# One core of a streaming encoder: the differential-attention layers rebuilt as one pipeline over all heads

## The reference, cut to what matters

```python
s = jnp.einsum('bqhmd,bkhmd->bhmqk', q, k, preferred_element_type=jnp.float32) * (A_DK ** -0.5)
s = s + jnp.transpose(bias, (2, 3, 0, 1))[None]      # T5 bias, constant from a distance of 128 on
if mask is not None:
    s = jnp.where(mask, s, NEG)                      # causal by chunks of 64
p = jax.nn.softmax(s, axis=-1)
a = p[:, :, 0] - lam * p[:, :, 1]  # (B,H,Q,K)
return jnp.einsum('bhqk,bkhe->bqhe', a.astype(v.dtype), v)
...
o = rms_norm(o, subln_g) * (1.0 - lam_init)          # per head, over its 128 columns
return o.reshape(B, S, A_V) @ w_o
```

## Time and profile before

| what | value |
|---|---|
| median of 3 runs | 4943.51 us (4939.37 to 5361.64) |
| span of the profiled execution, slowest core (core 0) | 5058.7 us |
| spans of cores 4 to 7 in that execution | 4925.3 to 4932.9 us |
| busy over core 0's span | PE 3998.5 us (79%), DVE 2351.2 (46%), ACT 1854.5 (37%), POOL 515.7 (10%) |
| chain that ended last | PE 57%, DVE 18%, issue 11%, ACT 8%, SPq 3% |

### The profile page before, as it was taken

The page is one execution under the profiler, slowest core; times in us unless marked ns, Lnnn a source line. Parts: engine busy times, 40 slices in busy tenths (PEclk is TensorE's granted clock), DMA queues, the critical chain, the costliest instruction groups (busy, mean ns, idle before and its releaser), DMA issues.

```text
span 5058.7 us, 80570 instructions; the slowest of 8 cores (4925.3 to 5058.7 us)
## 1 busy us (share of the span) xinstructions
PE 3998.5 (79%) x24866; PEld 2047.8 (40%) x25114; DVE 2351.2 (46%) x6161; ACT 1854.5 (37%) x4625; POOL 515.7 (10%) x1141
## 2 busy tenths in 40 slices
PE   2677777699996666999876777769999666699996
PEld 1444454344443323444444445434444333244442
DVE  1355655543343566433435665654333365733333
ACT  2365565612124335221236556562211343421111
POOL 0111111001011100010111111100101100000000
PEclk9789898799996777999878989879988676788887
DMA  6222222035441011454422222203544111034333
GB/s 108 50 38 35 41 47 37 5 51 74 69 65 13 10 18 19 69 72 68 50 47 39 35 39 46 40 5 51 74 60 63 21 12 18 13 51 63 55 51 98
DMA packets 379852, 229.87 MB, mean 45 GB/s; under 512 B 137024, under 2 KB 338160, under 8 KB 379440
## 3 DMA queue, kind: packets, MB, share of 16 engines
q0 software_dynamic: 282320, 169.08, 25.7%
q1 hardware_dynamic: 97120, 55.63, 4.0%
HBM read 350.01 MB, written 43.80 MB: 78 GB/s over the span
## 4 chain that ended last, share of the span: by engine, by line
PE 57%; DVE 18%; issue 11%; ACT 8%; SPq 3%; DVEq 1%; POOL 1%; DMA 0%; ACTq 0%; POOLq 0%
PE ps L1094 20%; PE ps L1070 19%; PE ps L753 3%; PE ps L791 3%; ACT ARENA L625 3%; DVE X L729 3%; PE ps L646 3%; SPq L119 3%; PE ps L597 3%; DVE ARENA L630 3%; PE ps L724 2%; ACT junk L945 2%; DVE FA L691 2%; PE ps L707 2%; DVE FA L938 2%
## 5 line engine op out<-in xcount | busy, mean ns | idle before, releaser
L625 ACT ACTIVATE ARENA<-ps,cfar 128x256 bf16<-128x256 f32 (+5 forms) x2400 | 1020.1, 516 | 813.7 <-PE ps L597 788.5
L1094 PE MATMUL ps<-RING,ARENA 128*128 128x512 bf16 x4272 | 1003.9, 397 | 60.6 <-DVE ARENA L1079 55.6
L1070 PE MATMUL ps<-ARENA,RING 128*128 128x512 bf16 (+1 forms) x5008 | 1001.4, 360 | 17.7 <-ACT ARENA L481 10.5
L1077 ACT ACTIVATE FA<-ps 128x512 f32<-128x512 f32 (+1 forms) x640 | 320.5, 521 | 1467.7 <-PE ps L1070 1422.0
L646 PE MATMUL ps<-ARENA 128*128 128x129 bf16 (+2 forms) x5696 | 532.8, 229 | 287.1 <-DVE ARENA L630 203.3
L1094 PEld LDWEIGHTS ps<-RING,ARENA 128*128 128x128 bf16 (+1 forms) x4352 | 440.1, 102 | 616.9 <-issue 255.7
L1098 DVE TENSOR_TENSOR X<-ps,X 128x512 f32<-128x512 f32 (+1 forms) x544 | 376.0, 691 | 667.8 <-PE ps L1094 667.8
L1079 DVE TENSOR_TENSOR ARENA<-FA 128x512 bf16<-128x512 f32 (+1 forms) x640 | 371.8, 598 | 644.1 <-ACT FA L1077 636.9
L1070 PEld LDWEIGHTS ps<-ARENA,RING 128*128 128x128 bf16 x5120 | 445.3, 102 | 534.1 <-issue 226.7
L646 PEld LDWEIGHTS ps<-ARENA 128*128 128x128 bf16 (+1 forms) x5696 | 394.8, 105 | 426.6 <-issue 397.9
L630 DVE TENSOR_TENSOR ARENA<-ARENA,E 128x256 bf16<-128x256 bf16 (+3 forms) x1344 | 324.2, 259 | 267.2 <-ACT ARENA L625 218.4
(11 more groups left out here) (84 smaller groups left out, 2424.8 us busy)
## 6 DMA issues: line engine op xcount, KB each, us to landing
RING<-mlp_w_up POOLq DMA_DIRECT2D x128, 512.0 KB, 6.2
RING<-mlp_w_down POOLq DMA_DIRECT2D x128, 512.0 KB, 12.0
a_k_prompt<-FA SPq DMA_DIRECT2D x256, 64.0 KB, 1.6
a_v_prompt<-FA SPq DMA_DIRECT2D x256, 64.0 KB, 1.7
RING<-a_w_qkv POOLq DMA_DIRECT2D x48, 256.0 KB, 5.2
X<-x_prompt SPq DMA_DIRECT2D x4, 2048.0 KB, 22.1
y_prompt<-FA SPq DMA_DIRECT2D x16, 512.0 KB, 2.6
ARENA<-cache_a_k POOLq DMA_DIRECT2D x16, 256.0 KB, 5.7
```

Source lines behind the costliest of these rows:

```text
L625: k.op(ACT, lambda: nc.scalar.activation(out=PT_ap(s, i2, 0, nk, c, c + w), in_=PS[bank][0:nk, c:c + w], func=AF.Exp, bias=cfar[0:nk, mp:m ...
L1070: k.op(PE, lambda: nc.tensor.matmul(PS[bank][:, 0:m1 - m0], RING[:, s, c * 256 + (fc % 2) * 128:c * 256 + (fc % 2) * 128 + 128], ARENA[:, ...
L1094: k.op(PE, lambda: nc.tensor.matmul(PS[bank][0:R, :], ARENA[:, M_AT + fc * 1088 + lc:M_AT + fc * 1088 + lc + R], RING[:, s, (fc % 2) * 102 ...
```

## The change

Layers B and the MLPs keep their code. In the A layers:

- Query tiles are taken in groups of three (0 to 2, 3 to 5, 6 to 8, 9 to 11) and two (12 and 13, 14 and 15), with the sample tile first: seven groups. A full step is 384 or 512 columns for each map; a head has 43 steps (before: 38).
- One ACT instruction makes the exponentials of both maps, over two neighbouring banks, with the scale 0.125 in it and no bias (a factor per map that cancels in the softmax). One DVE instruction masks both maps. There are three buffers for the probabilities.
- The accumulators of map 0 lie in bank 4, those of map 1 in bank 5. `finalize` reads them in PSUM: three small DVE instructions and two over the whole group form the difference times the row sum. What follows comes two, three, four and six steps later (`s2` to `s5`: squares on ACT, Ln and Exp, a product on POOL, transposes and a copy). One `reciprocal` of three columns replaces the normalization of each map.
- All 8 heads are one list of 344 steps. The projection of the next head and the output projections are generators in a queue (`bgq`); `run_bg` lets them emit work in proportion to the width of a step. They alternate between banks 6 and 7. The output projection of heads 0 and 1 runs in head 2, and so on; that of heads 6 and 7 in head 7 itself, tile by tile, with `emit_sq`.
- Q is projected in pieces of 512 columns; K and V two tiles per bank, with one copy, one cast each and one store each; K is transposed one piece later.
- The scratch row is written 128 times to HBM (2048 rows), `E` is loaded with one DMA on POOL's queue that casts it, and the DVE instruction that clears a part of it stands ahead of the one that clears `stats`.

```diff
+    PSALL = es.enter_context(nc.psum_tensor("ps", [128, 4096], F32))
+    PS = [PSALL[:, i * 512:(i + 1) * 512] for i in range(8)]
...
-    k.dma(SP, efd.ap()[:, 0:383], efs[:, 0:383], [efB], [efdB], k.semslot("efd_st"))
...
-        src = bass.AP(efd, 127 - p, [[384, 16], [1, 256]])
-        k.dma(SP, E32[p:p + 1, :, :], src, [efdB], [e32B], esem)
...
+    k.dma(POOL, E[:], bass.AP(efd, 127, [[383, 128], [128 * 384, 16], [1, 256]]), [efdB], [EB], esem)
+    k.op(DVE, lambda: nc.vector.memset(E[64:128, :, 0:64], 0.0), [EB], [EB])
...
     k.op(DVE, lambda: nc.vector.memset(stats[:, 0:34], 0.0), [], [ssB])
...
+    def bg_bank():
+        bg_rr[0] += 1
+        return 6 + bg_rr[0] % 2
...
+    def proj_A(j, h):
...
+        for g in range(5):
+            g0 = g * 512
+            g1 = min(g0 + 512, NTOK)
+            bank = bg_bank()
...
-            sg = stg_n[0] % NSTG
+                k.op(PE, lambda: nc.tensor.matmul(PS[bank][:, 0:g1 - g0], RING[:, sq, c * 128:(c + 1) * 128], hT_ap(c, g0, g1),
+                                                  start=(c == 0), stop=(c == 7)),
+                     [hTB[g], ringB[sq]], [PB[bank]], signal=(c == 7))
+                if c == 3 and g < 4:
+                    yield 4 * mm_ns(g1 - g0)
...
+            yield ktrans(A_CK + half * 512, [128] * 4, NTOK + half * 512, KTB[par][5], CKB)
+        late = None
+        for pr in range(9):
+            ts_ = [2 * pr, 2 * pr + 1] if pr < 8 else [16]
+            n2 = len(ts_)
...
+            for i, t in enumerate(ts_):
+                g = min(t // 4, 4)
+                for c in range(8):
+                    k.op(PE, lambda: nc.tensor.matmul(PS[bank][0:R, i * 256:i * 256 + 256], hT_ap(c, t * 128, t * 128 + R),
+                                                      RING[:, skv, c * 256:(c + 1) * 256],
+                                                      start=(c == 0), stop=(c == 7)), [hTB[g], ringB[skv]], [PB[bank]],
+                         signal=(c == 7 and i == n2 - 1))
...
+            sg = stg_n[0] % 3
...
+            if late is not None:
+                yield ktrans(*late)
+            late = (kt_o, [R] * n2, ts_[0] * 128, KTB[par][min(ts_[0] // 4, 4)], KTK[pr % 3])
...
+        groups = []
+        steps = [(NTOK + 128 * i, 128, 17 + i, 0, 0, ["P" if i == 7 else "F"]) for i in range(8)]
+        steps.append((2048, 64, 16, 0, 0, ["D"]))
+        groups.append(([16], steps))
+        for tl in ([0, 1, 2], [3, 4, 5], [6, 7, 8], [9, 10, 11], [12, 13], [14, 15]):
...
+    def oproj_A(j, pair, avail, after_tile):
+        rid, s = ring_next()
+        slots = [(2 * pair) % 3, (2 * pair + 1) % 3]
+        order = [16] + list(range(16))
+        for t in order:
+            while not avail(t):
+                yield 0
+            R = tile_rows(t)
...
+                after_tile(t)
+            yield 4 * mm_ns(512)
...
+        def run_bg(ns):
+            credit[0] += ns
+            while bgq and credit[0] > 0:
+                try:
+                    c = next(bgq[0])
+                    if c == 0:
+                        credit[0] = 0.0
+                        return
+                    credit[0] -= c
+                except StopIteration:
...
+        def emit_exp(n):
...
+            for nk, c0, c1 in segs:
+                src = PSALL[0:nk, b0 * 512:b0 * 512 + 1024].rearrange("p (s c) -> p s c", s=2)[:, :, c0:c1]
+                k.op(ACT, lambda: nc.scalar.activation(out=PTA_ap(i3, nk, c0, c1), in_=src, func=AF.Exp, scale=0.125),
+                     [PB[b0], PB[b0 + 1]], [PTA[i3]])
...
+        def emit_pv(n):
...
+                for idx, (sub, qi) in enumerate(items):
+                    (kcol, nk, vt, lo, hi, classes, coff) = sub
+                    qc, nq = q[qi]
...
+                    k.op(PE, lambda: nc.tensor.matmul(PS[4 + s][0:nq, qi * 129:qi * 129 + 129], PTA_ap(i3, nk, off, off + nq)[:, s, :],
+                                                      V_ap(kp, 0, nk, vt, 0, 129), start=(first and idx == 0),
...
+            if lastg:
+                finalize(h, gi)
+
+        def finalize(h, gi):
...
+            c3 = lambda c: fc(c).unsqueeze(2)
+            k.op(DVE, lambda: nc.vector.reciprocal(c3(0), acc(1)[:, :, 128:129]), [PB[5]], [fb["r"]])
+            k.op(DVE, lambda: nc.vector.tensor_scalar(c3(1), acc(0)[:, :, 128:129], SQEPS, None, ALU.mult), [PB[4]], [fb["s"]])
+            k.op(DVE, lambda: nc.vector.scalar_tensor_tensor(fc(2), fc(1), lamb[0:R, j, 2:3], fc(0), ALU.mult, ALU.mult),
+                 [fb["r"], fb["s"], lamB], [fb["c"]])
+            k.op(DVE, lambda: nc.vector.tensor_tensor(T, acc(1)[:, :, 0:128], c3(2).to_broadcast([R, G, 128]), ALU.mult),
+                 [PB[5], fb["c"]], [TB[r]])
+            k.op(DVE, lambda: nc.vector.tensor_tensor(O, acc(0)[:, :, 0:128], T, ALU.add), [PB[4], TB[r]], [OPB[r]])
...
+            def s2():
+                k.op(ACT, lambda: nc.scalar.activation(out=fc(3), in_=fc(1), func=AF.Square), [fb["s"]], [fb["w"]])
+                for qi in range(G):
+                    k.op(ACT, lambda: nc.scalar.activation(out=junk2[0:R, r, qi, :], in_=O[:, qi, :], func=AF.Square,
+                                                           accum_out=fin[0:R, r, 12 + qi:13 + qi]),
+                         [OPB[r]], [junk2B, fb["q"]])
...
+            def s3():
+                k.op(DVE, lambda: nc.vector.scalar_tensor_tensor(fc(5), fc(4), 1.0 / 128, fc(3), ALU.mult, ALU.add),
+                     [fb["q"], fb["w"]], [fb["v"]])
+                k.op(ACT, lambda: nc.scalar.activation(out=fc(6), in_=fc(5), func=AF.Ln), [fb["v"]], [fb["d"]])
+                k.op(ACT, lambda: nc.scalar.activation(out=fc(7), in_=fc(6), func=AF.Exp, scale=-0.5), [fb["d"]], [fb["d"]])
+
+            def s4():
+                k.op(POOL, lambda: nc.gpsimd.tensor_tensor(otok[0:R, r, 0:G, :], O, c3(7).to_broadcast([R, G, 128]), ALU.mult),
+                     [OPB[r], fb["d"]], [OTK[r]])
...
+            def s5():
+                bank = bg_bank()
+                pbf = PS[bank].bitcast(BF16)
...
+                k.op(DVE, lambda: nc.vector.tensor_scalar(OT_ap(h % 3, q[0][0], q[0][0] + w), pbf[:, 0:w], gsubT[:, j:j + 1], None, ALU.mult),
+                     [PB[bank], lamB], [OTA[h % 3][gi]])
+                done[(h, gi)] = True
+            n = it[0]
+            for d, f in ((2, s2), (3, s3), (4, s4), (6, s5)):
+                pending.append((n + d, f))
...
+            if n < N:
...
+                    tot = 0.0
+                    if h + 1 < 8:
+                        bgq.append(proj_A(j, h + 1))
+                        tot += PROJ_A_NS
+                    if h % 2 == 0 and h >= 2:
+                        bgq.append(oproj_A(j, h // 2 - 1, lambda t, h=h: (h - 1, grp_of_tile[t]) in done, None))
+                        tot += OPROJ_NS
+                    if h == 7:
+                        bgq.append(oproj_A(j, 3, lambda t: (7, grp_of_tile[t]) in done, emit_sq))
+                        tot += OPROJ_NS
+                    bg_total[0] = tot * 1.04
+                emit_exp(n)
+            run_pending(n)
+            if n >= 1:
+                emit_pv(n - 1)
+            if n + 1 < N:
+                if steps[n + 1][0] != steps[n][0]:
+                    drain_bg()
+                emit_qk(n + 1)
+            if n < N:
+                run_bg(bg_total[0] * act_ns[n] / head_act[steps[n][0]])
```

More of the change, by code:

```diff
@@ L21 @@
 EPS = 1e-6
+SQEPS = 1e-3
 NRING = 6
@@ L209, in _build @@
     A_OT = A_hT + 8 * NTOK
-    A_U = A_OT + 2 * NTOK
+    A_U = A_OT + 3 * NTOK
     KTW = NTOK + PAST
@@ L755, in q_chunks @@
                          [hTB[g], ringB[sq]], [PB[bank]], signal=(c == 7))
[L756 to L761 removed]
+                k.op(ACT, lambda: nc.scalar.activation(out=QT_ap(qp, 0, 128, c0, c1), in_=PS[bank][:, 0:c1 - c0], func=AF.Copy, scale=0.125),
+                     [PB[bank]], [QTB[qp]])
                 yield
@@ new lines, in layer_A @@
+        act_ns = [2 * 0.8 * width(n) + 93 for n in range(N)]
+        head_act = [0.0] * 8
+        for n in range(N):
+            head_act[steps[n][0]] += act_ns[n]
+        pending = []
+        fin_n = [0]
+        done = {}
+        it = [0]
+        bgq = []
+        credit = [0.0]
+        bg_total = [0.0]
+        def run_bg(ns):
[8 more added lines that the diff above has]
+                except StopIteration:
+                    bgq.pop(0)
```

446 lines of the change are left out of this document (248 added, 198 removed).

## The result

The changed kernel is faster: its time is 0.962 of the one before (interval 0.960 to 0.965), 4754.4 us against 4939.4, where 4575 us (4420 to 4750) had been forecast. The gain is 185 us, half of the forecast's 367. (The medians of all runs, 4827 and 5153 us, hold executions in which one die ran at a lower clock; only undisturbed ones are compared here.)

The account below looks back on a forecast made before the run. No engine was full; waits and the half clock took 304 us of a layer's attention. Attention falls to 638 us (157 and 156 less), starts gain 8 and 46: 4943.5 - 367 = 4576, called 4575 us, range 4420 to 4750.

Parts of the forecast that it names:

- start of the projection: First layer: writing, reading back and casting the table for `E` delays the start by 42 us, bounds 20 and 160.
- projection of head 0: Ahead of each A layer's attention: two banks hide the copies, 28 us, gaining 47 and 46 us; bounds 25 and 40.
- a layer's attention is then ... 491 us: PE's work in a layer's attention: 8 x 33.5 + 7 x 23.4 + 4 x 14.8 us, before and after alike.
- group ends: Accumulators held for DVE's reads: PE waits 1.0 us, 56 times a layer, 56 us; bounds 0.3 and 2.0.
- ACT's bursts: Two ACT bursts per group end make it 0.4 us late, 7 groups x 7 heads, 20 us a layer.
- the last transposes of K: Heads' ends: last transposed piece of K and masks queued behind DVE work, 2 us a head, 16 us.
- Head 7: 57 us of its own, plus 30 from squares of `X` between exponentials: 87 us, bounds 65 and 100.
- 81 ns for a pair of weight load and matmul: Value matmuls in the attention: at this gap, 6.3 us a head more and the kernel about 4675 us.
- Exponentials: ACT in each head: 14 of 1,024 columns at 1.06 us and 28 of 768 at 0.87, 39.5 us a head.
- Waits go by steps and groups: Rival, attention: chain of scores, exponential, mask, product sets the pace; heads keep 88 us, kernel about 4725; chance 0.21.
- The clock: Rival, attention: thinned PE work drops to 1.2 GHz; slower by 2% from share 0.48, 5260 us at 0.7; chance 0.04.
- Dense: Rival, attention: queued work covers most waits; a layer takes 554 us, the kernel about 4410; chance 0.19.

Follow-up runs that it names:

- The kernel with late squares: The changed kernel with each square of X emitted three tiles later, ACT's work in head 7 unchanged; 0.9475 of the time before the change, 4679 us.

## Why the prediction was wrong

The ledger of one A layer, forecast and first layer measured (us of core 4):

| term | forecast | measured |
|---|---|---|
| start of the projection, later by | 39 | 45.8 |
| projection of head 0 | 28 | 35.8 |
| attention | 638 | 718.4 |
| of it, PE at work | 491 | 570.5 |
| of it, PE idle | 147 | 147.9 |
| heads 0 to 6, at work and idle | 443 + 98 | 491.0 + 98.1 |
| head 7 and tail, at work and idle | 48 + 49 | 79.5 + 49.8 |

The differences, 7 + 8 + 80 in the first layer and 8 + 82 in the second, are 185; 367 less these is 182, and core 4 gained 183.4.

**The step that failed** is the first one of the sum: "a layer's attention is then ... 491 us", all columns at the 2.4 GHz level. The work was 80 us more. How much of that is the clock can be read from the stretches of this attention in which the trace grants 0.50, 129.7 us in 18 pieces; their sum:

```profile
sum 129.70, PE 102.26 PEld 51.83 DVE 40.36 ACT 56.09 POOL 8.77; mean PE 5.68 PEld 2.88 DVE 2.24 ACT 3.12 POOL 0.49
```

PE is busy there for 102.3 us and at full clock would be for half of that, so 51 of the 80 are the lower clock: 33 in head 7 and 18 in the other seven heads. The prediction priced the clock only as a rival that needed half of the work at 1.2 GHz (a tenth of it ran there, which by the rival's own formula is 100 us for the kernel); it left it out of its own case, though that case held 147 us of waits. The rows before the change could have warned: 597.3 us of busy time at 0.86 are some 514 us of work by the simple product, not 491. Over the attention 0.91 was granted, where above 0.95 had been expected.

The other 28 are size. They lie in heads 0 to 6 (some 30 us; head 7, which projects no keys and values, does its work in 46.6 us, where 48.3 had been taken). A step of 384 columns without a projection takes 0.71 us for its 1,542 columns (376.39 to 377.10 us on PE), 8% more per column than the wide step of the earlier trace rows, since six value matmuls in a row keep 73 ns each and eight keep 69. But for 28 such steps a head that is 1.5 us, about the 1.3 that had been allowed. The rest is in part how busy time is counted: the way of the last matmul before a wait is added to it (two of 512 columns ahead of a wait stand for 0.59 us, where their columns take 0.43), and PE waits some 180 times in a layer's attention. No run isolates it.

**Idle time** came out to the microsecond, and that is partly luck, for its terms did not: group ends 46 for 56; in heads 0 to 6 waits for exponentials of 1 us (7 with those put down to L1113) for the 20 of ACT's bursts, and waits for masks of 19, which with the last transposes of K had been given 16.

**Head 7.** With its tail it was forecast at 97 us and took 129.3, idle as forecast (49.8 us) and at work for 79.5 instead of 48. The 87 us had 14 squares holding ACT for 0.9 us each. The 16 full ones held it for 48.3 us, 3.0 each, because the additions they wait for stand behind output projections that stand behind products that wait for ACT: a circle, where a one-sided delay had been priced. The kernel with late squares shows what that is worth: 34 us of head 7, half of it clock, and 38 a layer, the largest gain of the single edits.

**Group ends** were nearly right: 42 waits of 1.1 us, 46.3 us, against 56 of 1.0. Of the 34 us a layer that the prediction estimated for the Trainium skill's advice to copy first (VectorE: DVE Perf Modes, "Rules for kernel authors"), 17 came: in this case the copies paid where DVE had room. The Trainium skill's 81 ns for a pair of weight load and matmul (TensorE: Matmul & The Clock Gate, "Back-to-back issue gap") was not reached, 69 to 73 were; yet the 4675 us that followed from it was nearer than 4575, for another reason.

**Exponentials** came at 0.81 and 1.02 us (forecast 0.87 and 1.06), and did not matter. **Start:** 42 us of delay were taken for the table and 44 (34.2 and 10.1) to 46 found; with bounds of 20 and 160, since no row had shown it, the closeness is luck. **Projection of head 0:** at clock 1.00 and yet 35.8 us, since PE is busy for 26.9 us (23.4 forecast) and idle for 8.9. In seven waits of about 0.9 us L822 waits for the copy of the pair before it (L832), 6.4 us in all. "With two banks" that copy was to be hidden, but the transposes of K between two pairs take a bank of the same alternation, so from the second pair on each pair meets the bank of the one before. The code and the rows show this; no run tested another order.

**Rivals.** "Waits go by steps and groups" (4725 us) came nearest, for a wrong reason: heads without an output projection took 75 to 79 us on core 4, not 88, and what made up the rest was clock and head 7. "The clock" named the mechanism that failed the forecast, for half of the work where it was a tenth. "Dense" is refuted by 148 us of idle time. The range's upper end lay 4 us below the result.

What stays open: why the clock stays high in one execution of a head and falls in another with the same instructions (head 3 at 0.93 and at 1.00), and why it falls behind one wait and not behind a longer one; in heads 0 to 6 this is worth 18 us a layer.
